# Statistics of the norms laid over four groups of 32 partitions, and spread back by TensorE

## The reference, cut to what matters

```python
def _rmsnorm(x, g):                         # 2 per layer and one at the end, over 1024 channels
    y = xf * lax.rsqrt(jnp.mean(xf * xf, axis=-1, keepdims=True) + EPS)
    return (y * g)

def _layernorm(x, g, b, eps=LN_EPS):        # gMLP: 4 groups of 128 channels; convolution: 1024 channels
    m = jnp.mean(xf, axis=-1, keepdims=True)
    v = jnp.mean(jnp.square(xf - m), axis=-1, keepdims=True)
    return (xf - m) * lax.rsqrt(v + eps) * g + b

# in _rwkv7_bidir, 8 heads of 64 channels
kk = hs(k * p['k_k'][i])
kk = kk / jnp.maximum(jnp.sqrt(jnp.sum(kk * kk, axis=-1, keepdims=True)), 1e-12)

# in _layer
h = _rmsnorm(x, p['norm1'][l]) * (1 + sc1) + sh1
x = x + gt1 * mixer(h)                      # layer 0: RWKV-7 || gMLP; layer 1: convolution
h = _rmsnorm(x, p['norm2'][l]) * (1 + sc2) + sh2
x = x + gt2 * _peer(h, l, p)
```

## Time and profile before

| | us |
|---|---|
| median of 3 runs (lowest, highest) | 3370.91 (3364.76, 3377.74) |
| the profiled execution | 3368.62 |
| its span, first to last instruction | 3366.8 |
| TensorE busy | 3143.5 (93%) |
| VectorE busy | 2177.3 (65%) |
| ScalarE busy | 1087.4 (32%) |
| GpSimd busy | 445.6 (13%) |
| mean granted TensorE clock | 0.954 |

### The profile page before, as it was taken

How to read it: one execution, slowest core, us unless ns; L and a number is a source line. 1 busy time by engine, 2 the same in 40 slices (tenths; PEclk the granted TensorE clock), 3 DMA queues, 4 the chain that set the end, 5 groups by cost and what they waited for, 6 DMA issues and landing times.

```text
span 3366.8 us, 64336 instructions
## 1 busy us (share of the span) xinstructions
PE 3143.5 (93%) x23958; PEld 2679.4 (80%) x23958; DVE 2177.3 (65%) x4215; ACT 1087.4 (32%) x1613; POOL 445.6 (13%) x194
## 2 busy tenths in 40 slices
PE   6979897999999999999998748999999999999998
PEld 3929584999998888887886424999998888887876
DVE  1654425795766767677844992695767676767843
ACT  2322222433233333333233333433233333332333
POOL 2500001563000000000000550563000000000000
PEclk7969799999999999999999868999999999999999
DMA  5451311443333333333332223343333333333332
GB/s 195 136 187 41 127 53 59 120 125 118 107 106 118 118 119 118 118 119 106 109 122 69 75 75 106 113 123 120 107 106 118 118 119 118 118 118 109 109 119 69
DMA packets 103838, 373.18 MB, mean 111 GB/s; under 512 B 12320, under 2 KB 14368, under 8 KB 103456
## 3 DMA queue, kind: packets, MB, share of 16 engines
q1 hardware_dynamic: 103712, 371.41, 35.0%
HBM read 369.53 MB, written 1.84 MB: 110 GB/s over the span
## 4 chain that ended last, share of the span: by engine, by line
PE 87%; DVE 6%; issue 3%; DMA 2%; ACT 1%; POOL 0%; DVEq 0%; SPq 0%; ACTq 0%
PE bank L1248 36%; PE bank L1330 32%; PE bank L1195 4%; PE bank L1017 3%; PE bank L960 2%; PE bank L1307 2%; DMA ring<-in_w_tiles 2%; PE bank L1322 1%; PE bank L983 1%; DVE arena L1859 1%; PE bank L999 1%; PE bank L951 1%; PE bank L1258 1%; DVE arena L1867 0%; DVE gated L1437 0%
## 5 line engine op out<-in xcount | busy, mean ns | idle before, releaser
L1248 PE MATMUL bank<-h_parts,split 128*128 128x384 f32 x6912 | 1270.1, 339 | 22.3 <-POOL h_parts L598 20.0
L1248 PEld LDWEIGHTS bank<-h_parts,split 128*128 128x128 f32 x6912 | 1198.6, 189 | 29.7 <-issue 17.5
L1330 PE MATMUL bank<-split,coef_parts 128*128 128x512 f32 x4608 | 1103.6, 395 | 10.2 <-DVE coef_parts L1786 10.2
L656 ACT ACTIVATE split<-ring 128x1024 fp32r<-128x1024 f32 x544 | 576.1, 1060 | 1365.9 <-PE bank L1330 694.3
L1330 PEld LDWEIGHTS bank<-split,coef_parts 128*128 128x128 f32 x4608 | 853.9, 189 | 184.0 <-DVE coef_parts L1786 10.7
L1779 DVE TENSOR_TENSOR split<-ring,split 128x1024 fp32r<-128x1024 f32 x440 | 536.2, 1219 | 142.8 <-ACT split L656 142.5
L591 POOL TENSOR_TENSOR split<-ring,split 128x1024 fp32r<-128x1024 f32 x104 | 262.9, 2532 | 682.0 <-ACT split L656 682.0
L1786 DVE TENSOR_TENSOR coef_parts<-gated,coef_parts 128x384 fp32r<-128x384 f32 x256 | 141.9, 555 | 279.5 <-ACT coef_parts L841 279.2
L1756 DVE TENSOR_TENSOR hot_i<-iota_h,routes_t 128x1536 f16<-128x1536 f16 x256 | 243.3, 950 | 10.7 <-ACT gated L816 10.7
L1827 DVE SCALAR_TENSOR_TENSOR gated<-bank,gated 128x384 f32 (+1 forms) x128 | 71.3, 557 | 140.8 <-PE bank L1307 140.8
L1770 DVE TENSOR_TENSOR hot_g<-hot_j,gate_t 128x384 f16<-128x384 f16 x512 | 158.3, 350 | 0.3
(11 more groups left out here) (246 smaller groups left out, 2540.8 us busy)
## 6 DMA issues: line engine op xcount, KB each, us to landing
ring<-in_e_u SPq DMA_DIRECT2D x256, 512.0 KB, 3.6
ring<-in_e_v SPq DMA_DIRECT2D x256, 512.0 KB, 3.5
ring<-in_w_tiles SPq DMA_DIRECT2D x183, 512.0 KB, 3.7
x_sb<-in_x_t SPq DMA_DIRECT2D x2, 768.0 KB, 6.6
y_t<-gated SPq DMA_DIRECT2D x4, 384.0 KB, 2.5
smallm<-in_mixer SPq DMA_DIRECT2D x1, 1375.5 KB, 7.9
smallm<-in_mixer SPq DMA_DIRECT2D x1, 1375.0 KB, 6.5
small<-in_small SPq DMA_DIRECT2D x1, 738.0 KB, 4.0
```

Source lines behind the costliest of these rows:

```text
L656: act.activation(split[:, 2 * p_ * D:(2 * p_ + 1) * D], ring[:, r * D:(r + 1) * D], ACT.Copy)\
L1248: mm = pe.matmul(out, part(e, x, c * P, (c + 1) * P), hp4[:, y, c, :], start=(c == 0 and x == 0 and y == 0), stop=(c == DC - 1 and x == 1))
L1330: mm = pe.matmul(bank[2 * b + hf][:, :], cp4[:, sl, x, b * P:(b + 1) * P], part(e, y, hf * 512, (hf + 1) * 512), start=False, stop=True, s ...
```

## The change

Where a statistic is the same on all 128 partitions, TensorE now writes it to 32 partitions only, and four such pieces stand side by side in one bank: for a norm the four quarters of the tokens (`TQ` = 96), for the gMLP its four groups, for kk the four pairs of heads. Root and reciprocal run once over 128 x 96 (norms), 128 x 384 (gMLP) or 128 x 385 (kk). Then four matmuls with 32 contracted rows, one for each group of 32 partitions, bring each piece back to all 128 partitions in four banks (`norm_spread` and its like); summing 32 equal rows with weights of 1/1024 multiplies by 1/32, which the root's scale and epsilon make up for. VectorE multiplies by these banks in place of an SBUF tile. The eight PSUM banks become slices of two tensors of four banks, so that one access pattern reads four banks. New waits: TensorE waits for the reciprocal before it spreads, VectorE for the spread.

```diff
@@ TensorE: norm_pe, and after it norm_spread
                 for c in range(DC):
                     pe.wait_ge(sq_ready, DC * u + c + 1)
-                    mm = pe.matmul(bank[0][:, 0:T], sm("mean_d"), sq3[:, c, :], start=(c == 0), stop=(c == DC - 1))
+                    for g in range(4):
+                        mm = pe.matmul(bank[0][32 * g:32 * g + 32, 0:TQ], sm("mean_d", 0, 32),
+                                       sq3[:, c, TQ * g:TQ * g + TQ], start=(c == 0), stop=(c == DC - 1),
+                                       skip_group_check=True)
                 mm.then_inc(ss_ready, 1)
+            def norm_spread(which=0):
...
+                pe.wait_ge(rs_ready, u)
+                for g in range(4):
+                    mm = pe.matmul(bank[4 + g][:, 0:TQ], sm("mean_d")[32 * g:32 * g + 32],
+                                   rstd[32 * g:32 * g + 32, 0:TQ], start=True, stop=True)
+                mm.then_inc(rs_spread, 1)
@@ ScalarE: the root
-                act.activation(root, bank[0][:, 0:T], ACT.Sqrt, bias=epsb[:, 0:1]).then_inc(rt_ready, 1)
+                act.activation(root[:, 0:TQ], bank[0][:, 0:TQ], ACT.Sqrt, bias=epsb[:, 0:1], scale=(32.0 / D) ** 2)\
+                   .then_inc(rt_ready, 1)
@@ VectorE: reciprocal and product
+            def norm_inverse(which):
...
+                dve.reciprocal(rstd[:, 0:TQ], root[:, 0:TQ]).then_inc(rs_ready, 1)
...
-                st.link(dve.reciprocal(rstd, root))
+                if (l, which) != (0, 0):
+                    norm_inverse(which)
+                dve.wait_ge(rs_spread, norm_n[0])
...
-                        st.mark(dve.tensor_tensor(sq3[:, c, :], x3[:, c, :], rstd, ALU.mult))
+                        st.mark(dve.tensor_tensor(quarters(sq3[:, c, :]), quarters(x3[:, c, :]), spread, ALU.mult))
...
+            norm_inverse(0)
             mod_add(0)
             mod_add(1)
             norm_dve(0, 0)
@@ TensorE: first norm
             norm_pe()
             mod_rows(0)
             mod_rows(1)
+            norm_spread()
             mod_turn(0)
@@ TensorE: gMLP
-                pe.matmul(half_bank(g)[:, 0:T], sm("mean_p"), gs[:, g, :], start=True, stop=True).then_inc(st_mm, 1)
+                pe.matmul(bank[4][32 * g:32 * g + 32, 0:T], sm("mean_p", 0, 32), gs[:, g, :], start=True, stop=True,
+                          skip_group_check=True).then_inc(st_mm, 1)
             pe.wait_ge(st_in, 4)
             mod_step(2, 0)
+            pe.wait_ge(gm_ready, 1)
+            for g in range(4):
+                pe.matmul(spread_bank(g)[:, 0:T], sm("mean_p")[32 * g:32 * g + 32], gs[32 * g:32 * g + 32, 0, :],
+                          start=True, stop=True).then_inc(gm_spread, 1)
@@ TensorE: kk
-                pe.matmul(bank[p][:, 0:TS], sm("head_sum"), tmp2[:, p, :], start=True, stop=True).then_inc(kk_ss, 1)
+                pe.matmul(bank[4][32 * p:32 * p + 32, 0:TS], sm("head_sum", 48, 80), tmp2[:, p, :], start=True,
+                          stop=True, skip_group_check=True).then_inc(kk_ss, 1)
             mod_turn(3)
+            pe.wait_ge(kk_ready, 1)
+            for p in range(4):
+                pe.matmul(bank[p][:, 0:TS], sm("pick")[32 * p:32 * p + 32], tmp1[32 * p:32 * p + 32, 0, :], start=True,
+                          stop=True).then_inc(kk_spread, 1)
...
                 for p in range(4):
+                    if d == 0:
+                        pe.wait_ge(kk_used, p + 1)
                     pe.matmul(bank[p][:, 0:TS], sm("w2", p * P, (p + 1) * P)[q], th[q], start=True, stop=True)\
@@ VectorE: kk
-            st.link(dve.reciprocal(tmp1, tmp1))
-            dve.scalar_tensor_tensor(nkk, nkk, -1.0, tmp1, ALU.mult, ALU.mult).then_inc(lw_sum, 1)
+            dve.reciprocal(tmp1[:, 0, :], tmp1[:, 0, :]).then_inc(kk_ready, 1)
+            for p in range(4):
+                dve.wait_ge(kk_spread, p + 1)
+                dve.scalar_tensor_tensor(nkk[:, p, :], nkk[:, p, :], -1.0, bank[p][:, 0:TS], ALU.mult, ALU.mult)\
+                   .then_inc(kk_used, 1)
```

109 lines of the change are left out of this document (69 added, 40 removed).

## The result

The changed kernel has a median of 3350.56 us (6 runs, 3338.87 to 3354.15) against 3371.14 us (6 runs, 3364.76 to 3377.74): ratio 0.9934, 95% interval 0.9914 to 0.9953, 20.6 us less. Its profiled execution has a span of 3349.4 us, 17.4 less than before. The forecast was 3348.5 us. The sum came out right, but several of its terms did not: the norms gave more than forecast, and kk and the convolution's LayerNorm cost 12 us where nothing was forecast.

A forecast was written before the change was run, and what follows sets the result against it. TensorE, nearly all in PEER's unchanged loops, was 87% of the chain of waits, so only short stages between could move. Terms -6.3, -4.4, -7.6, -3.6 and -0.5 gave -22.4 us, from 3370.9 to 3348.5 us; range 3338 to 3364.

The forecast's parts named there:

- A: Narrow product in the norms: 64 records of 96 columns overlap over four column groups, 2.2 us instead of 5.32.
- Rivals 2 and 3: Norm products: column groups do not overlap (3364 us, chance 0.10), or each record is drained first (3421 us, chance 0.03).
- rival 3: Norm products: narrow records drained before the next, 14.8 us each, decisive from 107 ns between starts; 3421 us, chance 0.03.
- B: Each norm: reciprocal over 96 columns takes 0.75 us, 1.8 us less; the root falls by some 0.25 us.
- C: Added spread in each norm: 8 records, costing 0.8 us at the high clock and 1.2 at the low one.
- D: VectorE's products with the bank no longer wait for GpSimd; gain of 1.0 us, 0 to 2.
- The first norm: Norm (0,0), at the kernel's start: 6.3 us less, with the steps of mod0 starting 4.0 us earlier.
- kk: Stage from head sums to chunk jobs: VectorE's gain is given to the ring of weight tiles; 0, -3 to +4 us.
- seven products of 0.67 us (two records of 333 ns): In kk: the LoRA products behind the spread end near 225.5 us, so the mod4 steps run near 226.
- The convolution's LayerNorm: Steps of mod11 now stand behind root, reciprocal and spread: 1.3 us ahead or 0.8 behind by the clock, taken as 0.
- low-clock case: In the convolution's LayerNorm: if the clock has not risen by the mod11 steps, they are behind by 0.8 us.
- Rival 1: Ring of weight tiles takes more than it gives: kk +4, convolution's LayerNorm +0.8; sum -14, 3357 us, chance 0.22.

The follow-up runs named there:

- e5: Changed kernel plus blocks of unread matmuls behind its last spread; the narrow product took 1.53 us over four column groups, 5.47 us in one.
- e4: Changed kernel, but in norms (0,1), (1,0) and (1,1) VectorE reads an SBUF copy of the spread made by ScalarE; median 3360.5 us.
- e3: Changed kernel plus matmuls of zeros in two TensorE waits at kk, before the last mod3 step and before the reciprocal wait; median 3338.9 us.
- e6: Changed kernel plus matmuls of zeros in the convolution's LayerNorm, at each variance chunk and before the reciprocal wait; three executions 3344.8 to 3351.5 us, a fourth 6156.
- e10: Changed kernel plus matmuls of zeros in the gMLP's two waits, before its reciprocal and before the last mod2 step; median 3348.3 us.

## Why the prediction was right, and where it was not

- **A, the narrow product: right, and for its reason.** Taken: 2.2 us, groups overlap. Measured: 1.84 us in norm (0,1), where its end came 3.4 us sooner after the last square, for 2.7; in the first norm it ends at 13.5 us, not at 14.0. e5 shows that the overlap of the column groups is the whole gain. Rivals 2 and 3 are out: 21 ns from start to start, where rival 3 needed 107.
- **B and C: right.** Reciprocal 0.75 us as worked out, spread 0.48 us at the high and 0.76 at the low clock; from the reciprocal's end to VectorE's product 0.61 us with both hops, where I had taken 0.8.
- **D: right mechanism, mis-sized.** Taken 1.0 in (0,1) and (1,1); measured 2.2 in each, the eight rests taking 8.36 us for 10.55, and e4 gives the same 2.2 back. I priced little more than the hole in GpSimd's rests. But the chain there is a loop: GpSimd's rest waits for ScalarE, which waits for VectorE, whose product was slowed by GpSimd's rest. Once the product is free, ScalarE's two instructions set the pace (1.05 us a chunk, hence 8.36 us for eight). These 2.4 us and 0.7 more from A in (0,1) are most of why (0,1) and (1,1) gave 11.6 us together, for 8.0; the rest of (1,1) gave 2.6, as forecast.
- **The first norm**: -5.0 at the projection's start and -5.9 at its second tile, for -6.3. The step of mod0 starts 4.2 us earlier as forecast (4.0); the row of steps gave some back (3.3 at the last).
- **kk: wrong, +9.0 for 0 (bounds -3 to +4).** The step that failed is "seven products of 0.67 us (two records of 333 ns)". Up to there the forecast held: with the lead of 7.2 us added back, the reciprocal ended at 218.75 (218.5 was forecast) and the spread at 220.5 (220.5). But 0.67 us was read at the high clock, from a profile in which the head sums, the turn and the products follow one another without a gap. The change made the sums 1.5 us for 4.36 and put a wait of 3.3 us behind the turn, and the products ran at 0.50 of the clock, 1.28 us each. So the first steps of mod4 ran at 230.9 in that count, for 226. What carries these 4.9 us to 9.0 at the end of the stage is rival 1's mechanism, which I had at +4: the next steps wait for tiles that the late ones free (they ran 6.0 and 8.4 us late), and nearly nothing is loaded meanwhile (DMA share 0.05). e3 gives the price of the low clock with all that hangs on it, 8.9 us.
- **The convolution's LayerNorm: wrong, +3.2 for 0.** I had a low-clock case with +0.8, but followed only the first two steps in it. The turn took 3.58 us for 1.84 and these steps came 0.9 us late, near that case; but they took 3.59 us for 1.90, so that their tiles were freed later, and the next two steps came 1.8 and 3.2 us late. From the spread on, e6 finds 3.2 us of clock.
- **Rival 1** had the right places and mechanism, but not the clock, and so less than half the price (4.8 for 12.2). The +12.2 of these two and +0.9 in the gMLP met -2.4 in the five norms together and -5.8 in stretches whose code did not change (-2.6, -2.9, -0.6, +0.2, +0.2, -0.1): 0.9 of the input projection's still belongs to the first norm, and the rest is of the size by which such stretches scatter in the table. So the median came within 2.1 us of the forecast partly by offsetting errors, and the statement to test was the one on the end of the kk stage: 6 to 8 us earlier was forecast, 1.75 later was measured.

## What to carry to other kernels

Statistics that are equal on all partitions can be laid over the four column groups of TensorE: the product is then a quarter as long, root and reciprocal shrink with it, and VectorE's operand moves to a bank, where GpSimd doesn't slow it. But before TensorE's work is made shorter at a place where it then waits, ask what stands behind the wait: its durations were read at a clock that went with TensorE working through, and weight tiles that it would free are not loaded. Independent work (here the next weight steps) belongs into that wait. In this kernel two such moves were worth more (31 us) than the change itself (21 us), though 15 of the 31 fill a wait that the kernel before had too.

## What the runs showed of the hardware that I had not expected

- TensorE's clock can fall while it is busy all the time: in block (e) of e5, 64 records of 32 rows in one row group without a gap, the granted clock was 1.00 at first (112 ns from start to start) and 0.50 to the end (213 ns), after 1.00 in each block before it.
- Fill keeps the clock up across one wait (0.90 for 0.50 in e3) and not behind another (1.00 beside the fill in e10, then 0.50 from 176 us on, with TensorE busy since its last step).
- The same code can get either clock: the turn behind the narrow head sums took 1.95 us in e5 and 3.58 in the changed kernel.
- At the high clock and with 96 columns streamed, records with weights of 32 rows and 128 columns start 112 ns apart in one row group and 28 ns apart over four; with weights of 128 rows and 32 columns it is 83 and 21 ns.
